# Token rows of two expert layers laid out by chunk of channels, with a copy of them in the second layer

## What is computed

```python
def hierarchical_moe(t, ...):                 # layer 1: EXPERT_FF = 256
    group_idx = jnp.argmax(group_probs, axis=-1)
    top_p, top_i = lax.top_k(jax.nn.softmax(in_group, axis=-1), 2)
    expert_ids = group_idx[:, None] * 8 + top_i
    ...                                       # tokens sorted by expert, in blocks
    hb = jax.nn.silu(xb @ w_gate[e]) * (xb @ w_up[e])
    return hb @ w_down[e]                     # then summed into the token's row with its gate

def second_block(x, ...):                     # layer 2: D_EXPERT = 512
    mix = _token_mixer(...)
    x = _layer_norm(DEEPNORM_ALPHA * x + mix, ln1_g, ln1_b)
    moe = _hier_moe(x, ...)                   # same routing, gated MLPs of width 512
    x = _layer_norm(DEEPNORM_ALPHA * x + moe, ln2_g, ln2_b)
```

## Time and profile before

| | |
|---|---|
| median of 3 runs | 2305.43 us (2302.77 to 2305.7) |
| profiled execution, its own time | 2309.89 us |
| span of its trace | 2307.7 us |
| PE busy | 2007.6 us, 87% |
| PEld busy | 1107.0 us, 48% |
| DVE / ACT / POOL busy | 795.5 / 382.0 / 80.6 us |
| mean granted TensorE clock | 0.938 of full speed |
| the placing product (L1380), layer 1 / layer 2 | 400.9 to 416.4 us / 1727.0 to 1742.5 us |

### The profile page before, as it was taken

One profiled execution on the slowest core, in us unless ns is written; L12 is line 12 of the kernel. 1 busy time (PEld: TensorE's weight loads), 2 busy tenths in 40 slices (PEclk: granted clock), 3 DMA queues, 4 the chain that ended last, 5 costly groups with the idle time before them and its releaser, 6 DMA issues.

```text
span 2307.7 us, 22803 instructions
## 1 busy us (share of the span) xinstructions
PE 2007.6 (87%) x8418; PEld 1107.0 (48%) x8418; DVE 795.5 (34%) x1472; ACT 382.0 (17%) x663; POOL 80.6 (3%) x84
## 2 busy tenths in 40 slices
PE   6999998887863999999999999999988988778781
PEld 4543335554432666656557776666554322223220
DVE  3336524112114355555554554232251101111105
ACT  2335531000001122232211111111000000000000
POOL 0001010200001000000000000000001000000001
PEclk9999998899886999999999999999988998999996
DMA  7715104699986211111011214222349999999993
GB/s 223 217 38 158 55 1 146 229 419 420 419 361 197 75 55 55 45 55 51 1 62 64 80 44 155 73 73 73 128 174 332 379 427 427 427 427 426 426 411 121
DMA packets 185573, 458.47 MB, mean 199 GB/s; under 512 B 30575, under 2 KB 134767, under 8 KB 159404
## 3 DMA queue, kind: packets, MB, share of 16 engines
q1 hardware_dynamic: 171916, 441.64, 51.0%
q0 software_dynamic: 7424, 16.06, 1.9%
q10 hardware_dynamic: 6176, 0.02, 0.1%
HBM read 434.20 MB, written 32.60 MB: 202 GB/s over the span
## 4 chain that ended last, share of the span: by engine, by line
PE 38%; issue 32%; DMA 23%; DVE 4%; SPq 2%; POOL 1%; ACT 0%; DVEq 0%; POOLq 0%; ACTq 0%
DMA stream<-in_w 12%; PE bank L1522 8%; DMA y_rows<-work 8%; PE bank L1389 6%; PE bank L451 3%; PE bank L391 2%; PE bank L1527 2%; PE bank L1402 2%; PE bank L416 2%; PE bank L1564 2%; PE bank L1390 2%; PE bank L466 1%; PE bank L395 1%; SPq L1304 1%; PE bank L479 1%
## 5 line engine op out<-in xcount | busy, mean ns | idle before, releaser
L1389 PE MATMUL bank<-stream,work 128*64 128x256 f32 (+1 forms) x1072 | 379.6, 513 | 72.4 <-DMA stream<-in_w 56.5
L1390 PE MATMUL bank<-stream,work 128*64 128x256 f32 (+1 forms) x1072 | 380.1, 513 | 0.0
L1389 PEld LDWEIGHTS bank<-stream,work 128*64 128x64 f32 x1072 | 150.8, 143 | 248.1 <-issue 173.1
L1522 PE MATMUL bank<-hT,stream 128*128 128x512 f32 x512 | 230.4, 593 | 1.7 <-DVE hT L1019 1.7
L1402 PE MATMUL bank<-stream,work 128*64 128x512 f32 x736 | 192.2, 676 | 39.4 <-DVE work L1476 39.4
L1390 PEld LDWEIGHTS bank<-stream,work 128*64 128x64 f32 x1072 | 150.7, 143 | 41.3 <-issue 25.7
L1473 DVE TENSOR_TENSOR work<-bank,work 64x256 f32<-64x256 f32 (+1 forms) x68 | 37.6, 554 | 341.6 <-ACT work L1445 341.3
L1522 PEld LDWEIGHTS bank<-hT,stream 128*128 128x128 f32 x512 | 93.4, 190 | 99.9 <-issue 98.0
L1480 DVE COPY work<-bank 128x512 f32<-128x512 f32 x34 | 23.5, 692 | 325.8 <-DMA y_rows<-work 173.2
L1402 PEld LDWEIGHTS bank<-stream,work 128*64 128x64 f32 x736 | 60.6, 153 | 146.7 <-issue 121.1
L1841 PE MATMUL bank<-stream 128*128 128x256 f32 x480 | 113.1, 383 | 3.3 <-ACT work L1866 3.3
(11 more groups left out here) (358 smaller groups left out, 2550.4 us busy)
## 6 DMA issues: line engine op xcount, KB each, us to landing
stream<-in_w SPq DMA_DIRECT2D x99, 2048.0 KB, 20.2
stream<-in_w_in SPq DMA_DIRECT2D x68, 512.0 KB, 4.2
stream<-in_w_gate SPq DMA_DIRECT2D x34, 1024.0 KB, 13.3
stream<-in_w_up SPq DMA_DIRECT2D x34, 1024.0 KB, 17.7
stream<-in_w_down SPq DMA_DIRECT2D x26, 1024.0 KB, 22.5
y_rows<-work SPq DMA_DIRECT2D x136, 128.0 KB, 14.6
stream<-in_w_in SPq DMA_DIRECT2D x16, 1024.0 KB, 5.4
stream<-in_w_out SPq DMA_DIRECT2D x2, 4096.0 KB, 15.5
```

The source lines that it names most:

```text
L1389: pe.matmul(bank[2 + s][other:other + 64, 0:m.ff], tokens, m.wg[slot][:, k, :], start=k == 0, stop=k == KD - 1)
L1390: last = pe.matmul(bank[2 + s][mine:mine + 64, 0:m.ff], tokens, m.wu[slot][:, k, :], start=k == 0, stop=k == KD - 1)
L1522: last = pe.matmul(bank[4 + c % 2][:, :], w_hg[:, c, k, :], hT[:, k, :], start=k == 0, stop=k == KD - 1)
```

## The change

In layer 1 VectorE writes the normed token rows by chunk: channel `q*8 + k` goes to column `k*128 + q` (`m.x_wide` is the same memory with the axes in that order). All that takes these rows afterwards (`turn_rows_pe`, `spread_pe`, `tokens_pe` on the gathered rows) takes 128 neighbouring elements in place of every eighth. In layer 2 the rows are wanted in `xres` order later, so ScalarE writes a copy by chunk into the first 4096 columns of the pool (`m.xg` and `m.xgT` lie there), one activation for each tile behind `ln_ready`, releasing `x_laid`. SP stores the rows to DRAM from this copy, behind `x_laid`. As copy and `m.xg`, `m.xgT` share memory, three waits come in: the first gather waits for the placing product (`xt_done`), VectorE's first write to `m.xgT` waits for the stores (`x_out`, a wait that stood in `scale_rows`), and TensorE's placing product waits for `x_laid`. Layer 2's clearing of `m.xg` is dropped.

```diff
--- before.py
+++ after.py
@@ -325,7 +325,7 @@
         route_in, fin_ready = sem("route_in"), sem("fin_ready")
         x_in = [sem(f"x_in{i}") for i in range(NT)]
         gains_in = sem("gains_in")
-        bias_in, spread, toep_in = sem("bias_in"), sem("spread"), sem("toep_in")
+        bias_in, spread, toep_in, x_laid = sem("bias_in"), sem("spread"), sem("toep_in"), sem("x_laid")
         w_pair_in = [sem("w_pair_in0"), sem("w_pair_in1")]
         latent_in, w_o_in, toep_rev_in = sem("latent_in"), sem("w_o_in"), sem("toep_rev_in")
         dve_own, act_own, pool_own = Count(sem("dve_own")), Count(sem("act_own")), Count(sem("pool_own"))
@@ -644,7 +644,7 @@
             pe.wait_ge(normed, NT + i + 1)
             for h in range(2):
                 for k in range(4):
-                    last = pe.transpose(bank[out_bank[i][h]][:, k * P:(k + 1) * P], moe1.x_rows[:, i, 4 * h + k:D:KD], ident[:, :])
+                    last = pe.transpose(bank[out_bank[i][h]][:, k * P:(k + 1) * P], moe1.x_rows[:, i, (4 * h + k) * P:(4 * h + k + 1) * P], ident[:, :])
                 last.then_inc(tr_done, 1)
 
         def logits_pe(pe, i):
@@ -1063,7 +1063,8 @@
                 m.y, at = cut(at, 2, D // 2)
                 m.place = m.y.rearrange("p a b -> p (a b)")[:, 0:2 * NT * SLOTS].rearrange("p (a s) -> p a s", s=SLOTS)
                 m.yg, at = cut(at, 2 * NT, D)
-                m.x_rows = m.yg[:, 0:NT, :] if layer == 1 else xres
+                m.x_rows = m.yg[:, 0:NT, :] if layer == 1 else work[:, pool_at:pool_at + NT * D].rearrange("p (a n) -> p a n", a=NT)
+                m.x_wide = m.x_rows.rearrange("p a (k q) -> p a q k", k=KD)
                 m.key, at = cut(at, NT, 2)
                 m.lg, at = cut(at, NT, LOGITS)
                 m.a1, at = cut(at, NT, EXPERTS)
@@ -1233,7 +1234,8 @@
         def clear_dve(dve, m):
 
             dve.memset(m.aa[:, NT, :], 0.0)
-            dve.memset(m.xg[:, :, :], 0.0)
+            if m.layer == 1:
+                dve.memset(m.xg[:, :, :], 0.0)
 
         def clear_list(sp, m):
             sp.dma_start(m.list_dram.rearrange("(e s) a -> e (s a)", s=SLOTS), no_tokens[0:EXPERTS + SPARE, :]).then_inc(list_zero, 16)
@@ -1342,6 +1344,8 @@
 
             pool.wait_ge(list_in, 16 * m.past + 16)
             pool.wait_ge(x_out, 16 * NT * (m.past + 1))
+            if m.layer == 2:
+                pool.wait_ge(m.xt_done, 1)
             for i in range(1, PAIRS_MAIN):
                 if i >= 2:
                     pool.wait_ge(m.xt_done, i - 1)
@@ -1369,15 +1373,17 @@
 
         def tokens_pe(pe, m, b):
             for k in range(KD):
-                last = pe.transpose(bank[k // 4][:, k % 4 * P:(k % 4 + 1) * P], m.xg[:, b, k:D:KD], ident[:, :])
+                last = pe.transpose(bank[k // 4][:, k % 4 * P:(k % 4 + 1) * P], m.xg[:, b, k * P:(k + 1) * P], ident[:, :])
             last.then_inc(m.xt_done, 1)
 
         def spread_pe(pe, m):
 
             pe.wait_ge(spread, m.past + 1)
+            if m.layer == 2:
+                pe.wait_ge(x_laid, NT)
             for k in range(KD):
                 for i in range(NT):
-                    last = pe.matmul(bank[6 + k // 4][:, k % 4 * P:(k % 4 + 1) * P], m.x_rows[:, i, k:D:KD],
+                    last = pe.matmul(bank[6 + k // 4][:, k % 4 * P:(k % 4 + 1) * P], m.x_rows[:, i, k * P:(k + 1) * P],
                                      m.place[:, 2 * i:2 * i + 2, :].rearrange("p a s -> p (a s)"), start=i == 0, stop=i == NT - 1)
             last.then_inc(m.xt_done, 1)
 
@@ -1486,6 +1492,8 @@
                 tokens_dve(dve, m, i, b)
                 pair(i, True, lambda: None)
 
+            if m.layer == 2:
+                dve.wait_ge(x_out, 32 * NT)
             tokens_dve(dve, m, 0, 0, 6)
             scale_rows()
             turns(dve, body)
@@ -2394,8 +2402,8 @@
             sp.dma_start(ln_row[1], A["ln1_b_2"].partition_broadcast(P).rearrange("p a n -> p (a n)")).then_inc(ln_in, 16)
             load_expert(sp, moe2, 0, 0)
             for i in range(NT):
-                sp.wait_ge(ln_ready, i + 1)
-                sp.dma_start(moe2.x_dram[i * P:(i + 1) * P, :], xres[:, i, :]).then_inc(x_out, 16)
+                sp.wait_ge(x_laid, i + 1)
+                sp.dma_start(moe2.x_dram[i * P:(i + 1) * P, :], moe2.x_rows[:, i, :]).then_inc(x_out, 16)
             load_expert(sp, moe2, 1, 1)
             load_gate_up(sp, moe2, 2, 2)
             sp.wait_ge(lg_done, 2)
@@ -2456,6 +2464,8 @@
             merge_act(act)
             for i in range(NT):
                 root_tile_act(act, 5, i)
+                act.wait_ge(ln_ready, i + 1)
+                act.activation(moe2.x_wide[:, i], xres[:, i, :].rearrange("p (q k) -> p q k", k=KD), ACT.Copy).then_inc(x_laid, 1)
             route_act(act, moe2)
             experts_act(act, moe2)
             for i in range(NT):
@@ -2499,7 +2509,8 @@
                 dve.wait_ge(h2_root, i + 1)
                 dve.reciprocal(stat[:, i:i + 1], stat[:, i:i + 1]).then_inc(*dve_own.up())
                 dve.wait_ge(*dve_own.now())
-                dve.tensor_scalar(moe1.x_rows[:, i, :], xres[:, i, :], stat[:, i:i + 1], None, ALU.mult).then_inc(normed, 1)
+                dve.tensor_scalar(moe1.x_wide[:, i], xres[:, i, :].rearrange("p (q k) -> p q k", k=KD), stat[:, i:i + 1], None,
+                                  ALU.mult).then_inc(normed, 1)
                 if i >= 1:
                     fold_dve(dve, 1, i - 1, gains[:, 2, :], out_bank[i - 1])
             fold_dve(dve, 1, NT - 1, gains[:, 2, :], out_bank[NT - 1])
@@ -2528,7 +2539,6 @@
             route_dve(dve, moe2)
 
             def scale_rows():
-                dve.wait_ge(x_out, 32 * NT)
                 for i in range(NT):
                     dve.tensor_scalar(xres[:, i, :], xres[:, i, :], ALPHA, None, ALU.mult).then_inc(*dve_own.up())
```

## The result

The changed kernel takes **2322.27 us** (median of 5, 2319.83 to 2325.86); the kernel before takes 2305.7 us (median of 5) on the same chip. The medians lie 16.6 us apart; the ratio is 1.0084, interval 1.0072 to 1.0095, which is 16.6 to 21.9 us. (The ratios in this document compare all runs of two kernels and are not quotients of two medians, which would give 1.0072 here.) The forecast was 2313.4 and its range ended at 2318. The direction was right, and the mechanism too, but the loss is about twice as large as forecast.

What follows compares the result with a forecast made beforehand. It took the chain last scatter, list load, gather of pair 1's rows to bound both expert layers' starts, with DMA full afterwards. Terms 0 + 7 + 1 = +8 us on 2305.43 gave 2313.4 us, range 2302 to 2318.

Steps and rivals of the forecast that it cites:

- The product (9.3 and 10.3 us foreseen): Placing product on TensorE with contiguous loads: 9.3 us in layer 1, 10.3 in layer 2, against 15.5 before.
- Its direct worth, 0: The shorter placing product gains 0 in both layers, as long as the gather of pair 1's rows does not move.
- That the earlier `gu_done` lets weights in ahead of the list: Pair 0's earlier release issues weights at about 416 and 1746 to 1747, so the whole list load runs beside them.
- Layer 1 ... I take 0: Layer 1's list lands between 424 and 428, the gather at 429 to 433 against 432.0: -2 to +1, taken as 0.
- weights queued from 417 to 427: Layer 1's 4 MB of weights beside the list load, taken to pass in 10 us at 419 GB/s.
- Layer 2 ... +7 (up to +10): Layer 2's list lands at about 1765 to 1769, the gather at 1771 to 1774 against 1764.8: +7 us, up to +10.
- Case A: The forecast itself: list load held until most queued weights have passed, +6 to +12, 2311 to 2317 us; chance 0.45.
- Weights queued until 1768 to 1770: Layer 2's 8 MB of weights beside the list load, taken to pass in 20 us at 427 GB/s.
- VectorE "+1": VectorE's stepped write of `x_rows` in layer 1, about 1.8 us a tile, delays layer 1's list by 1 us (0.5 to 1.3).
- ScalarE, "I take 0": ScalarE's four copies, 1.06 to 1.9 us each, delay loads of experts 1 and 2: 0 to +1, taken as 0.
- The sum: Total of the forecast's terms, 0 + 7 + 1 = +8 us, for a median of 2313.4 us.

Runs made afterwards that it cites:

- e5: Changed kernel with the placing product done twice over, every other edit kept: 2305.2 us, ratio 1.0006 to the kernel before.
- e2: Changed kernel with each expert layer's first weight reload held on SP until the first gather has landed: 2305.27 us, ratio 1.0012 to the kernel before.
- e3: Kernel before, without the change, with each expert layer's first weight reload held until the first gather has landed: 2300.52 us, ratio 0.9986.
- e12: Kernel before with the list load cut in two, pair 1's column first and its gather waiting for that alone: 2297.21 us, ratio 0.9964.
- e1: Changed kernel with each expert layer's first weight reload held on SP until the token list has landed: 2306.66 us, ratio 1.0010 to the kernel before.
- e4: Kernel before, without the change, its placing product leaving out token tiles 2 and 3, so half as long: 2321.35 us, ratio 1.0079.
- e6: Kernel before with the change made in layer 1 alone: 2309.49 us, ratio 1.0022.
- e7: Kernel before with the change made in layer 2 alone: 2317.18 us, ratio 1.0062.
- e8: Kernel before with the first weight reload held until pair 1's gather has landed, in layer 1 alone: 2303.02 us, ratio 0.9995.
- e11: Changed kernel with the list load cut in two, pair 1's column first and its gather waiting for that alone: 2315.38 us, ratio 1.0045 to the kernel before.

## Why the prediction was wrong

- **The product (9.3 and 10.3 us foreseen): right.** 9.0 and 9.3 us, at 192 ns a load once the clock is at 2.4 GHz.
- **Its direct worth, 0: right, as long as the gather comes last.** e5 does the work twice and loses nothing; e2 is not faster than e3. It is no property of the product: in layer 2 of e12 the gather no longer comes last.
- **That the earlier `gu_done` lets weights in ahead of the list, and that this is what counts: right**, by e1, e4 and e5, which separate it from every edit of the change.
- **"Layer 1 ... I take 0" failed.** It cost 4.3 us at the transposes (35.4 - 31.1) in the changed kernel, 7.3 in e6, and 5.1 us of e6's time. The step priced the list load alone. The last scatter, issued at 415.80, landed only at 423.10 (7.3 us against 3.24): 4.1 us that no term held. And "weights queued from 417 to 427" took their rate for their whole time. They lost 3.4 us at the start (45 and 86 GB/s from 416 to 420) and ended near 429.5, the list at 431.8.
- **"Layer 2 ... +7 (up to +10)" failed.** +13.3 in the changed kernel, 14.3 us of e7's time. From the placing product to the transposes the last scatter took 1.8 us more (9.86 for 8.03), the list load 18.1 more (21.62 for 3.53), the gather 6.9 less (4.37 for 11.23). Case A's rule, that the list ends behind the queued weights, held; its date was wrong. "Weights queued until 1768 to 1770" put nothing ahead of the weights, but the last layer-norm rows were still in the queue: the first row of weights passed after 1751, over 4 us behind its issue, and the last at about 1772. Then the list had nearly all of its own work before it: it landed 2.8 us behind the bulk of the weights, at 1774.45, where the forecast let it land with them or ahead of them, at 1765 to 1769. That the gather would then be nearly alone (4.37 us) was the cheapest value on offer, and right.
- **VectorE "+1": about right.** The placing product starts at 401.49 for 400.88, 0.6 us later. Over all fourteen traces the eight kernels with the stepped write start it at 400.6 on average, the six without at 399.7, with a spread of over 2 us in either. A stepped write takes 1.35 us where 1.8 were taken.
- **ScalarE, "I take 0": too low.** Its copies take 1.98 us each, and SP's loads of expert 1, which wait for them, are issued 16.5 us ahead of the placing product in place of 18.2. The loads behind them, the layer-norm rows last, so run longer beside the scatters: in layer 2 the last scatter takes 8.7 to 10.3 us in the eight kernels with the copies and 6.0 to 8.6 in the six without them, 2.4 us more on average. (That it is the later loads that do this is the likely link, not tested by itself.) In the changed kernel it is part of layer 2's loss; in e1 and e5 the time hardly shows it.
- **The sum.** +8 was 0 + 7 + 1; the layers alone measured 5.1 + 14.3. The step that failed most is layer 2's list load, priced as if the weights had an empty queue and the list would land with them: its term was short by 6 to 7 us. Then comes layer 1's, by 4 to 5.

The **traces** differ by 12.4 us (2320.1 - 2307.7), less than the medians. The profiled execution of the kernel before was a long one (2309.89 against a median of 2305.7), and it shows where: from the end of layer 1's last down product to the placing product of layer 2 it takes 1020.6 us (706.37 to 1726.98), the changed kernel 1015.2 (713.40 to 1728.57). One row of each for 1100 to 1400 us (the clock is the third number from the end), before:

```profile
1100.00:1400.00 300.00, 291.04 (x1117) 204.29 (x1116) 157.32 (x250) 45.63 (x65) 0.00 (x0) 0.98 0.18 55
```

and after:

```profile
1100.00:1400.00 300.00, 291.05 (x1165) 207.47 (x1164) 158.83 (x251) 46.70 (x67) 0.00 (x0) 1.00 0.17 55
```

The granted clock is 0.98 against 1.00. It isn't the change's: e8, which has none of it, has 1.00 and 1014.8 us, and e6, which has it in layer 1, 0.98 and 1018.7.

**Open.** Why the split between last scatter and list varies in layer 1 (e6 against the changed kernel); why a list load needs 3 to 4 us from issue to its first packets beside weights, and why the first weights of layer 1, with nothing but scatters beside them, pass at 45 and 86 GB/s. How much of layer 2's loss the layer-norm rows ahead of the weights make was not tried (issuing them elsewhere would tell). The cut list in the changed kernel together with held weights wasn't tried, nor the change on top of e12, where layer 2 has room for it.

## What to carry to other kernels

When a change makes an engine finish earlier, ask first which transfers its semaphore releases and what small transfers are still under way: here some 6 us saved on TensorE in each layer bought 19 us of loss. Ask as well what still stands in the queue ahead of the released transfers. Price a small transfer beside a full stream by its elements on one DMA engine times the time of one row of the stream, and add the start (here 3 to 4 us); where that exceeds the stream's own length, it ends behind the stream. So cut from a many-element load the part that somebody waits for, and send it first: that alone made the kernel before 0.36% faster (interval 0.22 to 0.51%).

## What the runs showed of the hardware

- Two queues share a DMA engine by one packet each in turn: 123 for 123 in 4 us, the ones of 4 bytes, the others but for 16 of 16 KB. The same list load took 3.5 us alone and 21.6 to 23.1 us beside 8 MB of weights.
- A list load issued on busy DMA engines needed 3 to 4 us to its first packets (e11, layer 2), against 0.8 to 1.8 us on empty ones (before, layer 2); the weights of layer 1 passed at 45 and 86 GB/s over 416 to 420 us, their first four microseconds, and at 393 GB/s and more behind that.
- Two loads of 512 KB in rows of 4 KB, beside scatters, were still draining at 47 to 246 GB/s over 1746 to 1752 us, and no row of the weights queued behind them, issued at 1746.54, passed before 1751.
- A stationary f32 operand with a step of 32 bytes takes 335 ns to load against 192 at 2.4 GHz, and 338 against 333 at 1.2 GHz; VectorE's write with steps 1.35 us against 0.75 for 1024 elements, ScalarE's 1.99 against 1.06.
